# Scan rounds: the first x pair of groups 1 and 2 is projected two slots ahead, in slots 8 and 9 of the round in front

## The reference, cut to what matters

```python
rest = h @ w_in[:, D_INNER:]                       # x, B, C and dt; z = h @ w_in[:, :D_INNER]
xbc = silu(dwconv(rest[..., :CONV_DIM], conv_w, conv_b))   # 5 taps over the tokens
xs = xbc[..., :D_INNER].reshape(b, l, N_GROUPS, HEADS_PER_GROUP, SSM_HEAD_DIM)
y_f, s_f = ssd_scan(xs, dt[:, :, 0], A[0], bm, cm, h0_f, with_out)
y_b, s_b = ssd_scan(flip(xs), flip(dt[:, :, 1]), A[1], flip(bm), flip(cm), h0_b, with_out)
y = y_f + flip(y_b) + d_skip * xs
```

## Time and profile before

| what | value |
|---|---|
| median of 3 runs | 1860.78 us (1860.24 to 1864.98) |
| the profiled execution | 1859.74 us, its span 1857.9 us |
| mean granted TensorE clock | 0.994 |
| busy over the span | PE 97%, DVE 61%, ACT 49%, POOL 5% |
| last projection rows of group 0 end | 684.7 us |
| round 0, from its first bc to that of round 1 | 697.36 to 761.43 us |
| round 1, to the first bc of round 2 | 761.43 to 827.83 us |

### The profile page before, as it was taken

How to read it: one execution, slowest core, us unless ns; L and a number is a source line. 1 busy time by engine, 2 the same in 40 slices (tenths; PEclk the granted TensorE clock), 3 DMA queues, 4 the chain that set the end, 5 groups by cost and what they waited for, 6 DMA issues and landing times.

```text
span 1857.9 us, 25616 instructions
## 1 busy us (share of the span) xinstructions
PE 1795.4 (97%) x10135; PEld 1316.4 (71%) x10136; DVE 1131.3 (61%) x1453; ACT 917.6 (49%) x1436; POOL 100.7 (5%) x81
## 2 busy tenths in 40 slices
PE   6989999999999999899999999999999999999997
PEld 5976788888888887687888566665666666655563
DVE  3266476765657797688867565565555555555644
ACT  3235573222246646577756455444454445444433
POOL 1000000000000123323300000000000000000000
PEclk9999999999999999999999999999999999999999
DMA  9466215666355532122259999999999999999995
GB/s 355 146 212 243 91 46 182 211 196 201 139 193 193 164 94 69 37 78 68 92 190 355 386 390 407 409 412 414 410 407 411 412 413 409 409 412 412 413 407 239
DMA packets 182459, 498.22 MB, mean 268 GB/s; under 512 B 10348, under 2 KB 62908, under 8 KB 167996
## 3 DMA queue, kind: packets, MB, share of 16 engines
q1 hardware_dynamic: 181760, 495.93, 70.6%
q10 hardware_dynamic: 571, 0.57, 0.1%
HBM read 495.42 MB, written 1.05 MB: 267 GB/s over the span
## 4 chain that ended last, share of the span: by engine, by line
PE 77%; DVE 8%; DMA 5%; ACT 4%; SPq 3%; issue 2%; POOL 0%; ACTq 0%; DVEq 0%; POOLq 0%
PE bank L991 12%; PE bank L992 11%; PE bank L993 11%; PE bank L1681 9%; PE bank L1673 4%; PE bank L1256 4%; PE bank L1258 4%; PE bank L1257 4%; DMA raw<-in_moe_gu_w_dram 3%; SPq L854 2%; DVE ar L3045 2%; PE bank L1356 2%; PE bank L1357 2%; PE bank L1358 2%; SPq L849 1%
## 5 line engine op out<-in xcount | busy, mean ns | idle before, releaser
L2685 DVE TENSOR_TENSOR lo<-raw,hi 128x1024 fp32r<-128x1024 f32 x182 | 216.9, 1222 | 171.1 <-ACT hi L1975 169.0
L2666 DVE TENSOR_TENSOR lo<-raw,hi 128x1024 fp32r<-128x1024 f32 x172 | 212.8, 1243 | 146.8 <-ACT hi L1955 144.5
L1955 ACT ACTIVATE hi<-raw 128x1024 fp32r<-128x1024 f32 x156 | 164.7, 1059 | 259.1 <-PE bank L1258 172.7
L1975 ACT ACTIVATE hi<-raw 128x1024 fp32r<-128x1024 f32 x182 | 187.0, 1057 | 146.5 <-DMA raw<-in_moe_gu_w_dram 55.5
L991 PE MATMUL bank<-hi,xg_t 128*128 128x512 f32 x448 | 182.3, 407 | 3.4 <-ACT ar L2488 1.4
L992 PE MATMUL bank<-lo,xg_t 128*128 128x512 f32 x448 | 175.2, 391 | 0.0
L993 PE MATMUL bank<-hi,xg_t 128*128 128x512 f32 x448 | 174.9, 390 | 0.0
L2685 DVE TENSOR_TENSOR lo<-ar,hi 128x1024 fp32r<-128x1024 f32 x94 | 112.1, 1222 | 90.4 <-ACT hi L1975 89.1
L991 PE MATMUL bank<-hi,hth 128*128 128x512 f32 x400 | 160.1, 400 | 2.0 <-DVE lo L2685 1.9
L992 PE MATMUL bank<-lo,hth 128*128 128x512 f32 x400 | 156.0, 390 | 0.0
L993 PE MATMUL bank<-hi,htl 128*128 128x512 f32 x400 | 155.8, 390 | 0.0
(11 more groups left out here) (400 smaller groups left out, 3328.9 us busy)
## 6 DMA issues: line engine op xcount, KB each, us to landing
raw<-in_moe_gu_w_dram SPq DMA_DIRECT2D x126, 1024.0 KB, 16.0
raw<-in_moe_down_w_dram SPq DMA_DIRECT2D x60, 1024.0 KB, 16.3
ar<-in_moe_gu_w_dram SPq DMA_DIRECT2D x59, 1024.0 KB, 17.9
out_slot<-in_moe_gu_w_dram SPq DMA_DIRECT2D x39, 1024.0 KB, 15.6
ar<-in_moe_down_w_dram SPq DMA_DIRECT2D x33, 1024.0 KB, 16.1
raw<-in_ada_w_dram SPq DMA_DIRECT2D x14, 2048.0 KB, 9.1
raw<-in_ffn_gu_w_dram SPq DMA_DIRECT2D x22, 1024.0 KB, 5.2
raw<-in_ffn_down_w_dram SPq DMA_DIRECT2D x22, 1024.0 KB, 4.9
```

What stands on the lines that cost most here:

```text
L1955: A_(hi[:, p % SPL, :], raw[:, slot(u), (p % 2) * PIECE:(p % 2 + 1) * PIECE], ACT.Copy).then_inc(hi_ready, 1)
L1975: A_(hi[:, q % SPL, :], m_raw(i)[:, (q % 2) * PIECE:(q % 2 + 1) * PIECE], ACT.Copy).then_inc(m_hi, 1)
L2666: TT(lo[:, p % SPL, :], raw[:, u, h * PIECE:(h + 1) * PIECE], hi[:, p % SPL, :].bitcast(F32), ALU.subtract).then_inc(done, 1)
L2685: TT(lo[:, q % SPL, :], src[:, (q % 2) * PIECE:(q % 2 + 1) * PIECE], hi[:, q % SPL, :].bitcast(F32), ALU.subtract).then_inc(m_lo, 1)
```

## The change

For groups 1 and 2 (`EARLY = 2`), the first x pair is projected in slots 8 and 9 of the round in front of the one where it was: group 1's behind the projection of group 0, group 2's in round 0. Slots 0 and 1 of rounds 0 and 1 then have no projection; the second pair and B and C stay in slots 2 to 5. ACT does the `conv_in` of blocks 0 and 1 in slot 0 for these groups, before in slot 1. DVE does their convolutions in slots 1, 2, 4, 5, 6, 7, before in 2 to 7. The two fills of 3 in slot 9 of `project(0, ...)` and the three fills behind `project` in slots 7, 8 and 9 of round 0 go. `used_by` follows the new order. Groups 0 and 3 are as before.

```diff
+        EARLY = 2
         def used_by(g, k):
+            ahead = max(0, k - 8)
             if g < 0:
-                return 2 * S_GRP + min(k, 6)
-            if g == 0:
-                return 2 * S_GRP + 6 + min(k, 6)
+                return 2 * S_GRP + min(k, 6) + ahead
+            if g < EARLY:
+                a = 2 * S_GRP + (8 if g == 0 else 14 + 10 * (g - 1)) + min(max(0, k - 2), 4)
+                return a + (max(0, k - 6) if g > 0 else 0) + (ahead if g < EARLY - 1 else 0)
             a = 2 * S_GRP + 12 + 10 * (g - 1)
...
                 if k < 4:
-                    proj("x", g, k // 2, k % 2)
+                    if k >= 2 or not 1 <= g <= EARLY:
+                        proj("x", g, k // 2, k % 2)
                 elif k < 6:
                     proj("bc", g, 0, k - 4)
                 elif g > 1:
                     proj("z", g - 1, (k - 6) // 2, k % 2)
-                if k == 9 and g == 0:
-                    fill(bank[2][:, 0:256], 3)
+                elif k >= 8:
+                    proj("x", g + 1, 0, k - 8)
                 if k >= 5:
                     to_tok(g, k - 5)
                 if k == 9:
-                    if g == 0:
-                        fill(bank[2][:, 0:256], 3)
                     cb(g)
...
-                if g == 0 and k >= 7 or g == N_GROUPS - 1 and k in (4, 5):
+                if g == N_GROUPS - 1 and k in (4, 5):
                     late_fill(g, 3)
...
-                for i in {1: (0, 1), 3: (2, 3), 5: (4, 5), 8: (6, 7)}.get(k, ()):
+                for i in {(0 if 1 <= g <= EARLY else 1): (0, 1), 3: (2, 3), 5: (4, 5), 8: (6, 7)}.get(k, ()):
...
-                if 2 <= k <= 7:
-                    conv(g, k - 2)
+                at = (1, 2, 4, 5, 6, 7) if 1 <= g <= EARLY else (2, 3, 4, 5, 6, 7)
+                if k in at:
+                    conv(g, at.index(k))
```

More of the change, by code:

```diff
@@ L2312, in project @@
                     return
-                for i in {1: (0, 1), 3: (2, 3), 5: (4, 5), 8: (6, 7)}.get(k, ()):
+                if k in (7, 9) and g > 1:
+                    zs(g - 1, (k - 7) // 2)
+                for i in {(0 if 1 <= g <= EARLY else 1): (0, 1), 3: (2, 3), 5: (4, 5), 8: (6, 7)}.get(k, ()):
                     if i >= 2:
@@ L2317, in project @@
                         conv_in(g, i)
-                if k in (7, 9) and g > 1:
-                    zs(g - 1, (k - 7) // 2)
                 if k >= 5:
```

## The result

| | before | after |
|---|---|---|
| median | 1861.43 us, 8 runs (1859.23 to 1864.98) | 1867.96 us, 8 runs (1866.76 to 1870.77) |
| ratio, 95% interval | | 1.0039 [1.0029, 1.0048] |
| span of the profiled execution | 1857.9 us | 1865.1 us |
| last decay sums of group 0 to bc of round 0 | 11.59 us | 17.98 us |
| round 0, round 1, round 2 | 64.07, 66.40, 65.39 us | 62.70, 68.14, 65.39 us |

The change makes the kernel 6.5 us (0.39%) slower by the medians. A profiled execution is one draw, so I compare stretches inside it. They begin at the first matmul of the last decay sums (685.77 us before, 685.52 after), which the change doesn't touch, and go from bc to bc. They differ by 6.76 us. The spans differ by 7.2: the changed kernel is 0.25 us ahead where the stretches begin and loses another 0.7 behind round 2, so the expert stage returns nothing.

A forecast was written before the change was run, and what follows sets the result against it. TensorE was taken to bind slots 0 to 3 of a round, DVE and ACT slots 4 to 9 of round 0. Terms of +2.3 us plus 3.4 for the clock gave +5.7 on 1860.78: 1866.5 us, range 1861.5 to 1871.5.

The forecast's parts named there:

- (a): End of group 0's projection: group 1's pair moved there brings bc of round 0 later, +7.05 us.
- (b): Slots 0 and 1 of round 0: -10.95 us for two calls gone, +5.35 us new wait for ACT's state_out.
- (f): TensorE's clock behind both new waits: half rate in slots 2 and 3, +3.4 us in all, bounds 0 to 6.8.
- (c): DVE's shifted convolutions in round 0: time saved in slot 3 falls into a wait for TensorE, worth 0.
- (d): Slots 8 and 9 of round 0: group 2's first pair comes in, fills go, TensorE becomes dense, +1.95 us.
- (e): Slots 0 and 1 of round 1: -10.95 us for two calls gone, +9.85 us wait behind a longer chain.
- One low stretch each: Each new wait of 5.35 and 9.95 us brings one half-rate clock stretch on slots 2 and 3, 1.7 us lost.
- Faster: Rival, chance 0.08: ACT's chain does not end last in slots 0 and 1; -12.9 us, 1847.9 us.
- The cheap clock: Rival, chance 0.18: new waits come, but low stretches fall into them or an old one disappears; +0.7 to +3.5 us.

The follow-up runs named there:

- lean with open waits: Changed kernel with ACT's conv_in behind state_out, no weight pieces in slot 0, no fill of 4 before round 0, no fills in waits: 1859.68 us, ratio 0.9994.

## Why the prediction was right

It said 1866.5 us in a range of 1861.5 to 1871.5, slower by over 0.3% with 0.56; the median is 1867.96. Step by step, in stretches of the profiled executions:

| step | predicted | measured |
|---|---|---|
| (a) up to bc of round 0 | +7.05 | +6.39 |
| (b) from there to `state_lat` of round 0 | -10.95 + 5.35 = -5.60 | -5.61 (wait 5.25) |
| (f) clock, and (c), slots 2 to 7 of round 0 | +1.7 + 0 | +2.13 |
| (d) slots 8 and 9 | +1.95 | +2.11 |
| (e) slots 0 and 1 of round 1 | -10.95 + 9.85 = -1.10 | -0.69 (wait 10.10) |
| (f) clock, rest of round 1 | +1.7 | +2.43 |
| sum | +5.7 | +6.76 |

- **(a)** was over by 0.66 us. I had both to_tok behind TensorE at 690.39. In fact the program order puts slot 8's behind the first projection, so the projection began at 689.58. From there to bc it took 13.92 us for the 14.0 predicted. The prediction also says that the two removed fills bring nothing. In the kernel before they bring 1.08 us, as the run without the fills shows; in the changed kernel TensorE is dense there, so nothing of this entered the sum.
- **(b)** From bc to `state_lat` took 7.79 us, 7.8 predicted. Two errors inside cancel: seg started 1.03 us after bc, not 0.55, since a weight piece stands ahead of it, as I had it in (e) and not here; and the two conv_ins took 2.28 us, not 2.7. That the term came out within 0.01 us is therefore luck. The experiment without the fill of 4 shows the DVE work ahead of seg as what binds there.
- **(c)** From the wait for `state_out` to the bc of slot 7 the lag grew by 2.13 us, of which the 3.9 us at half clock behind the restart are 1.9. DVE in slots 4 to 7 binds as before, and the run with the old convolution slots shows no difference.
- **(e)** The chain was 12.55 us instead of 12.3: the second row of gated took 1.99 us next to POOL's copies, 1.23 before, and the two conv_ins again took 2.28 us and not 2.7, which hid part of it.
- **(f)** was the right mechanism at too small a size: 3.4 taken, 1.9 + 2.3 measured. "One low stretch each" was right; the first lasted 3.9 us past the restart and the second 4.7, where the stretches of the earlier trace rows had 3.4. They were longer than that in all, 6.9 and 10.2 us, and began 3.0 and 5.5 us before the restart. The Trainium skill ("TensorE: Matmul & The Clock Gate", Part 1: The HAM clock gate) says that an idle TensorE is put back to half rate; both waits here were, and the bounds that followed from the two stretches of the trace, 0 to 6.8, held.
- **The rivals.** Faster did not come: ACT's order decides, as the run with conv_in behind state_out shows: 6.0 us come back there, and with the pieces out of slot 0 and the waits filled the kernel is faster than before, if by 3 us and not by 12.9. The cheap clock was wrong for both waits, and the low stretch of before behind the wait at 807.55 did not go either: it is there at 814.06. No further one came.

What stays open is how much of the differences of 1 to 2 us among the six kernels with conv_in behind state_out is their edits and how much is where the clock fell in their runs.

## What to carry to other kernels

Work moved off one engine's busy slots leaves the other engines' queues as they were: before moving it, list what stands ahead of the releaser of the next wait, in program order. If part of that list (here two conv_ins and the weight pieces, 3.6 to 4.3 us of the two waits) is wanted later than the releaser, move it behind in the same edit. Without that, the freed slots can turn into waits: here 10.95 us of work left twice, and waits of 5.25 and 10.10 us came in its place. And a fill costs nothing only as long as it stands in a wait: look for the engine that would be late if it went, and for the clock of the work behind it.

## What the runs showed of the hardware that was not expected

- **The same wait costs the clock in one run and not in the next.** At TensorE's wait for the second conv_in in rounds 1 and 2, all between 1.57 and 1.71 us, the clock fell in round 1 in nine of the thirteen kernels, among them before (807.55) and after (814.06), and stayed full in four, among them the one with conv_in behind (810.31); in round 2 it stayed full in every kernel but one. That one is the first row, behind 1.70 us at 872.54; the second row is the same wait, 1.70 us at 875.07, in the kernel with the fill of slot 7 kept:

```profile
872.00:878.00 6.00, 5.46 (x36) 5.32 (x38) 5.32 (x8) 5.86 (x12) 1.65 (x1) 0.72 0.03 8
```

```profile
875.00:881.00 6.00, 5.93 (x56) 5.63 (x57) 5.32 (x7) 5.86 (x12) 1.69 (x1) 1.00 0.01 3
```

- **Shorter waits are not safer.** It fell after 1.36 us in the kernel with fills of 9 and 18 (749.03), and stayed full after 2.94 us with conv_in behind (712.10).
- **Nor does the length of a wait tell how long the clock stays low behind it.** Past the restart it was low for 3.9 us behind a wait of 5.25 (changed kernel) and 4.7 behind 5.27 (group 1's pair alone), for 5.3 and 5.0 behind two of 5.82 (no piece in slot 0; lean with open waits), 3.3 behind 7.79 and 4.7 behind 10.10; behind waits of 1.36 to 2.13 us, where it fell, for about 3.4.
- **Where a row of DVE with no bank among its operands overlaps one of POOL, the one that starts second is longer.** In the changed kernel the second row of gated starts 0.13 us after POOL's copy and takes 1.99 us, 1.23 before; mul at 711.90, which starts inside a POOL row of 711.40, takes 1.52 us, 0.69 elsewhere. The weight piece at 701.04 in the DVE rows above, 0.23 us behind the start of a POOL copy, takes 1.95 us, the next one 1.21. In the kernel before it is once the other way round: mul at 768.43 starts 0.13 us ahead of POOL's copy and keeps its 0.69 us, and the copy takes 1.46 us instead of 1.04. The masked cb at 698.61 there, which reads a bank, takes its usual 0.76 us beside a POOL copy from 698.39. These are places of this case; no run moves a POOL row to test it. The first two rows are of the changed kernel, the others of the kernel before:

```profile
767.88 1.04 POOL L950 TENSOR_TENSOR ar<-ar 128x512 f32<-128x512 f32 x1 [6.09 <-PE bank L1424]
768.01 1.99 DVE L3126 TENSOR_TENSOR ar<-ar,raw 128x1024 f32<-128x1024 f32 x1
```

```profile
768.43 0.69 DVE L3096 TENSOR_TENSOR ar<-ar,raw 128x512 f32<-128x512 f32 x1 [1.64 <-ACT ar L2338]
768.56 1.46 POOL L946 TENSOR_TENSOR ar<-ar 128x512 f32<-128x512 f32 x1 [9.47 <-PE bank L1420]
```
